# Where the moving tiles start and in which order the products of a k tile are issued; a loop written out

## The reference

```python
# first block
proj = rms_norm(x, g_mix) @ w_in                   # 2048 x 9216
...
x = x + merged @ w_out
h2 = rms_norm(x, g_ff)
x = x + square(relu(h2 @ w_ff1)) @ w_ff2           # 2048 x 8192, 8192 x 2048
# second block
h = modulate(rmsnorm(x, norm1_g), sh1, sc1)
q, k, v, f, hy = split_projection(h @ w_in_2)      # 2048 x 5120
kc, vc = split(hc @ w_in_2[:, 1024:3072], 2)       # the context, 256 rows too
...
x = x + g1 * (y @ w_out_2)
gate, up = split(modulate(rmsnorm(x, norm2_g), sh2, sc2) @ w_up, 2)   # 2048 x 11264
x = x + g2 * ((gelu(dwconv(gate)) * up) @ w_down)                     # 5632 x 2048
```

## Time and profile before

| | us |
|---|---|
| three runs, median | 2763.87 |
| three runs, lowest and highest | 2761.56, 2767.94 |
| the profiled execution, its own time | 2765.6 |
| its span, from the first to the last instruction | 2763.8 |
| TensorE busy | 2683.0 |
| VectorE busy | 1899.2 |
| ScalarE busy | 1178.4 |
| mean granted clock of TensorE | 0.983 |
| read from HBM | 553.57 MB |

### The profile page before, as it was taken

How to read it: one execution, slowest core, us unless ns; L and a number is a source line. 1 busy time by engine, 2 the same in 40 slices (tenths; PEclk the granted TensorE clock), 3 DMA queues, 4 the chain that set the end, 5 groups by cost and what they waited for, 6 DMA issues and landing times. The chain is left out here.

```text
span 2763.8 us, 51119 instructions
## 1 busy us (share of the span) xinstructions
PE 2683.0 (97%) x21116; PEld 2587.0 (94%) x21116; DVE 1899.2 (69%) x2409; ACT 1178.4 (43%) x1228; POOL 0.2 (0%) x4
## 2 busy tenths in 40 slices
PE   7999999998999999999999999999899999999998
PEld 7989999998999999999999899859899999999998
DVE  7778877886888788888872236756666665656566
ACT  4666554434543444343432233333444443434343
POOL 0000000000000000000000000000000000000000
PEclk9999999999999999999999999999999999999999
DMA  7666666675888888878743253404455554545453
GB/s 281 223 226 220 212 232 237 237 244 191 268 269 278 274 280 273 279 274 275 272 171 100 99 166 126 154 20 145 146 192 189 184 192 160 186 166 185 167 184 106
DMA packets 282686, 558.37 MB, mean 202 GB/s; under 512 B 10408, under 2 KB 16841, under 8 KB 282057
## 3 DMA queue, kind: packets, MB, share of 16 engines
q1 hardware_dynamic: 282104, 553.60, 58.5%
q10 hardware_dynamic: 400, 2.11, 0.3%
HBM read 553.57 MB, written 2.10 MB: 201 GB/s over the span
## 5 line engine op out<-in xcount | busy, mean ns | idle before, releaser
L882 DVE TENSOR_TENSOR WL<-RAW,WH 128x1024 fp32r<-128x1024 f32 x840 | 1018.9, 1223 | 699.8 <-ACT WH L477 692.1
L477 ACT ACTIVATE WH<-RAW 128x1024 fp32r<-128x1024 f32 x840 | 890.9, 1063 | 1404.1 <-PE PS L1591 1280.2
L1589 PE MATMUL PS<-XH,WH 128*128 128x256 f32 x4288 | 1215.9, 284 | 41.1 <-issue 27.5
L1590 PE MATMUL PS<-XL,WH 128*128 128x256 f32 x4288 | 1205.6, 281 | 0.0
L1591 PE MATMUL PS<-XH,WL 128*128 128x256 f32 x4288 | 1204.9, 281 | 0.0
L1589 PEld LDWEIGHTS PS<-XH,WH 128*128 128x128 f32 x4288 | 815.2, 190 | 46.9 <-issue 33.3
L1590 PEld LDWEIGHTS PS<-XL,WH 128*128 128x128 f32 x4288 | 815.6, 190 | 1.2 <-issue 0.7
L1591 PEld LDWEIGHTS PS<-XH,WL 128*128 128x128 f32 x4288 | 815.0, 190 | 0.0
L1589 PE MATMUL PS<-HH,WH 128*128 128x256 f32 x1728 | 482.8, 279 | 0.4 <-DVE X L1192 0.4
L1590 PE MATMUL PS<-HL,WH 128*128 128x256 f32 x1728 | 482.3, 279 | 0.0
L1591 PE MATMUL PS<-HH,WL 128*128 128x256 f32 x1728 | 482.2, 279 | 0.0
(11 more groups left out here) (240 smaller groups left out, 1888.2 us busy)
## 6 DMA issues: line engine op xcount, KB each, us to landing
RAW<-in_w_ff SPq DMA_DIRECT2D x128, 1024.0 KB, 5.4
RAW<-in_w_in SPq DMA_DIRECT2D x112, 1024.0 KB, 5.1
RAW<-in_w_up SPq DMA_DIRECT2D x88, 1024.0 KB, 4.8
adab<-in_ada_w SPq DMA_DIRECT2D x128, 512.0 KB, 4.7
RAW<-in_w_down SPq DMA_DIRECT2D x44, 1024.0 KB, 5.0
ada1b<-in_ada_w SPq DMA_DIRECT2D x64, 512.0 KB, 5.9
RAW<-in_w_out SPq DMA_DIRECT2D x32, 1024.0 KB, 5.0
RAW<-in_w_oa SPq DMA_DIRECT2D x8, 1024.0 KB, 5.1
```

The source lines that it names most:

```text
L477: A(WH[:, c.base % 2, hs], RAW[:, c.base % SLOTS, hs], ACT.Copy).then_inc(hi_done, 1)
L882: tt(WL[:, b, hs], RAW[:, c.base % SLOTS, hs], WH[:, b, hs].bitcast(f32), ALU.subtract)\
L1589: MM(out[:, f, :], wh, xh, start=first and f % 2 == 0, stop=False, skip_group_check=True)
L1590: MM(out[:, f, :], wh, xl, start=False, stop=False, skip_group_check=True)
```

## The change

Three things. The tiles that move through TensorE (`XH`, `XL`, `HH`, `HL`) start 32 bytes later, on odd multiples of 32 bytes, and with them all that shares their place; `CON` moves by 64 bytes to make room. `ws` issues, for each of the three products of a k tile, the four column blocks in the order 0, 2, 1, 3 before it goes to the next product. The loop of the second feed-forward is written out on all four engines: eight more calls of `ff2_step` with fixed chunk numbers.

```diff
@@
-FF2_ITERS = (STEPS2 - 3) // 2
@@
-        XH = at("XH", [P, KC, T], 80 * K + 64, f32r)
-        XL = at("XL", [P, KC, T], 96 * K + 64, f32r)
-        HH = at("HH", [P, 2, FT, T], 112 * K + 64, f32r)
-        HL = at("HL", [P, 2, FT, T], 120 * K + 64, f32r)
-        NT = at("NT", [P, KC, T], 112 * K + 64)
-        CON = 128 * K + 64
+        XH = at("XH", [P, KC, T], 80 * K + 96, f32r)
+        XL = at("XL", [P, KC, T], 96 * K + 96, f32r)
+        HH = at("HH", [P, 2, FT, T], 112 * K + 96, f32r)
+        HL = at("HL", [P, 2, FT, T], 120 * K + 96, f32r)
+        NT = at("NT", [P, KC, T], 112 * K + 96)
+        CON = 128 * K + 128
@@
-        t1 = 112 * K + 64
+        t1 = 112 * K + 96
@@
-        fcl = at("fcl", [P, TT, 2 * T], 80 * K + 64)
+        fcl = at("fcl", [P, TT, 2 * T], 80 * K + 96)
...
@@ SP; ScalarE, VectorE and TensorE alike
-            with sp.Fori(0, FF2_ITERS) as i:
-                ff2_step(Place(2, i, 2))
-                ff2_step(Place(3, i, 2))
+            for j in range(2, STEPS2 - 1):
+                ff2_step(Place(j))
@@ ws
-                for f in range(FT):
-                    cs = slice(f * P, (f + 1) * P)
-                    wh, wl = WH[:, b, kk, cs], WL[:, b, kk, cs]
-                    MM(out[:, f, :], wh, xh, start=first and f % 2 == 0, stop=False, skip_group_check=True)
-                    MM(out[:, f, :], wh, xl, start=False, stop=False, skip_group_check=True)
-                    ins = MM(out[:, f, :], wl, xh, start=False, stop=last, skip_group_check=True)
+                for n, (w, x) in enumerate(((WH, xh), (WH, xl), (WL, xh))):
+                    for f in (0, 2, 1, 3):
+                        ins = MM(out[:, f, :], w[:, b, kk, f * P:(f + 1) * P], x, start=first and n == 0 and f % 2 == 0,
+                                 stop=last and n == 2, skip_group_check=True)
```

More of the change, by code:

```diff
@@ L246, in build_program @@
         SM = at("SM", [P, KC, T], AR + 8 * K)
-        fcl = at("fcl", [P, TT, 2 * T], 80 * K + 64)
-        fcd = at("fcd", [P, 2, P], 84 * K + 64)
-        fU = at("fU", [P, FNG, 2 * T], 88 * K + 64)
+        fcl = at("fcl", [P, TT, 2 * T], 80 * K + 96)
+        fcd = at("fcd", [P, 2, P], 84 * K + 96)
+        fU = at("fU", [P, FNG, 2 * T], 88 * K + 96)
         KS = at("KS", [P, 2, 5, HW], AR + 24 * K)
@@ L252, in build_program @@
         YS = at("YS", [P, 4, HW], AR + 48 * K)
[L253 to L258, removed]
+        hSD = at("hSD", [P, 2, 2, TT, HW], 80 * K + 96)
+        dec = at("dec", [P, 2, TT, HW], 96 * K + 96)
+        Ef = at("Ef", [P, TT, 6 * P], 104 * K + 96)
+        pz = at("pz", [33, T], 110 * K + 96)
+        w1h = at("w1h", [33, 64], 111 * K + 96)
+        w2h = at("w2h", [64, 64], 111 * K + 96 + 512)
         w3h = at("w3h", [64, 2048], t1)
@@ L861, in _ @@
             ff2_step(Place(1))
-            with act.Fori(0, FF2_ITERS) as i:
-                ff2_step(Place(2, i, 2))
-                ff2_step(Place(3, i, 2))
+            for j in range(2, STEPS2 - 1):
+                ff2_step(Place(j))
             for s in range(4):
@@ L1550, in _ @@
             ff2_step(Place(1))
-            with dve.Fori(0, FF2_ITERS) as i:
-                ff2_step(Place(2, i, 2))
-                ff2_step(Place(3, i, 2))
+            for j in range(2, STEPS2 - 1):
+                ff2_step(Place(j))
             c, q = Place(C_END - 4), Place(Q_END - 4)
@@ L1999, in _ @@
             ff2_step(Place(1))
-            with pe.Fori(0, FF2_ITERS) as i:
-                ff2_step(Place(2, i, 2))
-                ff2_step(Place(3, i, 2))
+            for j in range(2, STEPS2 - 1):
+                ff2_step(Place(j))
             for s in range(SLOTS):
```

## The result

| | before, us | after, us |
|---|---|---|
| median of the timed runs | 2767.82 | 2751.60 |
| lowest, highest of 12 runs each | 2759.04, 2772.18 | 2730.04, 2757.25 |
| the profiled execution, its own time | 2765.6 | 2750.69 |
| its span | 2763.8 | 2748.9 |

The ratio after to before is 0.9943 [0.9925, 0.9962]: faster by 0.57%, some 16 us, where 92 us had been forecast and the range ended at 2737. Here is the page of the kernel after: busy time by engine, the clock in 40 slices, and two of the costliest groups.

A forecast was written before the change was run, and what follows sets the result against it. TensorE's own matmul pace was taken as the bound. From the profiled 2765.6 us, -59.5 (parity), -2.7 (`tok`), 0 (order) and -29.7 (loop) sum to -91.9, giving 2673.7; the median, 1.7 lower, 2672 us; range 2640 to 2737.

The forecast's parts named there:

- (1) Parity: `ws` matmuls with XH, XL, HH, HL: odd multiples of 32 bytes give 113.3 ns instead of 116.7, -59.5 us.
- three paces: `ws` matmuls in the earlier trace: XH at 116.7 ns apart, MH at 117.7, CH at 113.3.
- rival C: `ws` matmuls: odd tiles share two paces, half at 113.3 and half at 117.7 ns; 2713 us, chance 0.14.
- (2) `tok`: 672 `tok` matmuls with XH: odd place gains 4.0 ns each, -2.7 us.
- (3) The order: Product order in `ws`, bank changing after each matmul: 0 us, bounds -24 and -4 us against +48 us.
- D: `ws`: the order helps too, down to the weight loads' pace, 112 ns; 2644 to 2648 us, chance 0.14.
- E: `ws`: 16,000 added bank changes cost time; at 3 ns each without parity gain 2782 us, chance 0.07.
- (4) The loop: Second feed-forward's loop written out: stalls and half clock at three boundaries go, -29.7 us.
- The cover: VectorE, ScalarE and DMA work behind the matmuls: still hidden at the faster pace, priced 0.
- The rule against it: Skill's statement on TensorE: separate read ports, loads steal no bandwidth; tile places would change nothing, leaving the loop's gain alone.
- rival B: Whole kernel: neither parity nor order does anything, only the loop gains; 2734 us, chance 0.16.

## Why the prediction was right or wrong

**(1) Parity, -59.5 us forecast, +16 us measured: wrong, and this is the step that failed.** The price per matmul was real, 113.3 for 116.7, and so were the three paces. The variable was read wrongly. `CH` and `XH` in the earlier trace rows differ in parity, but also in their distance from the weights, 192 and 32 modulo 256. I took the one property that the change alters, and put the new `XH` with `CH`. It came to lie at 64, whose usual pace is 117.8. `MH`, as odd as `CH` and at 117.7 in the earlier trace rows, stood against it from the start. The prediction priced it for all matmuls only as the lower bound of this term, "it would cost 18,048 x 1.0 = +18 us" (rival C took it for half of them), and gave that outcome neither a rival nor a chance. With the loop it makes 2764 - 30 + 18 = 2752, and 2751.6 was measured. So close a match is luck, since that sum starts 4 us below the median of before in the same comparison and leaves out what `MH` and `CH` lost. A bound that has a row of its own in the same trace is a rival.
By the paces, the moved tiles cost 18,048 x 1.1 = 20 us, `MH` and `CH` at 120.0 instead of 113.3 or 117.8 another 4 to 8, and that is more than the 16 measured. TensorE also ran at half clock for less time in the profile with the tiles alone (68 us in all) than in that of before (98 us), but this differs from execution to execution, also 91 us with the order alone. Over all their timed runs the mean granted clock is 0.986 with the tiles alone and 0.984 before, some 11 us less at half clock; at 116.7 and 213 ns a matmul that is worth about 5 us, an estimate, which brings the 24 to 28 down to 19 to 23. The measured interval ends at 22.

**(2) `tok`, -2.7 us forecast, nothing gained.** In the profile after, the starts with `XH` still lie 233.3 ns apart; spans of nine with `CH` mostly give 226.7 (228.9 in the earlier trace rows). Here as there parity was not the variable, and the distance was: with `XH` the starts of `tok` lie 233.3 ns apart at 32, 64 and 112, 228.9 at 192 and 226.7 at 0. So the best of these distances for `tok` is the one at which `ws` takes 120.0.

**(3) The order, 0 forecast: right.** 1.0002 [0.9991, 1.0012] puts it between -2.5 and +3.3 us for 16,000 more changes of bank, at most 0.2 ns each. The upper bound of 3 ns (+48 us) and the lower one, the pace of the loads (-24 us), are both gone, and rivals D and E with them.

**(4) The loop, -29.7 us forecast, -31.8 measured: right.** The windows of the kernel after show straight code at clock 1.00 where the earlier trace rows had 0.96, and the stalls by "issue" fell by 17.7 us in six pieces. The half clock that followed them is gone too: 39 matmuls at each of three places, at 213 ns instead of 116.7, are another 11 us, and the two make 29 of the 31.8, within the interval.

**The cover: right.** VectorE at 1899.7 us and ScalarE at 1178.3 did not change, and even at 113.3 nothing waited anew.

**The rule against it.** The prediction set the trace against the Trainium skill (TensorE: Matmul & The Clock Gate, step 1 of "Step-by-step: what each phase is for"), by which the streaming operand and the loads have ports of their own. By that rule place would change nothing, and the time would have been rival B's 2734. The runs bear out neither B nor my reading: with every other engine still, place alone moved the pace from 113.3 to 123.3 ns. Whatever the ports are, the two operands don't go independently of their distance.

**Of the rivals,** none gave the result. C had the two paces right, but between 113.3 and 117.8 at equal shares; the kernel after has 19 of some 907 groups at the better one. Had it been priced with `MH`'s pace alone, its 2752 would have been in the range.

**What stays open:** what picks the pace where a distance has two; what sets the pace where the two moving tiles lie at different distances; why two of the 12 timed executions of the kernel after took 2730 us, which a better share of 113.3 would explain but which no profile caught; and what in the chip has a period of 256 bytes.

## What to carry to other kernels

Where TensorE's pace is the time, measure the pace of a matmul stream as the distance between starts, and compare it across tiles that differ only in place: here the distance between the moving tile and the weights, modulo 256 bytes, is worth up to 4% of a whole kernel, for no instruction at all. Sweep the distance in a small kernel of TensorE alone before moving anything, with repeats, since a distance may have two paces, and for each form of matmul, since `ws` and `tok` have different best distances; and list what else tells two rows apart before taking one property for the cause. A loop on TensorE whose branch back takes 6 us, as the one with 1152 matmuls and as many loads did here, costs some 10 us a turn and is worth writing out.

## What the runs showed of the hardware that was not expected

- The pace of float32r matmuls of 256 columns with a load of weights each depends on the distance between the operands in SBUF modulo 256 bytes, from 113.3 ns (112 bytes) to 123.3 ns (4 bytes), with all other engines idle. Which paces a distance has does not depend on the absolute place, tried at five places of the weights and with the moving tiles 40 K further. This holds where all moving tiles keep the same distance.
- With 512 moving columns and the activations stationary, the same distances give 226.7 ns (0), 228.9 (192) and 233.3 (32, 64 and 112).
- Distances of 32, 64 and 192 bytes have two paces each, chosen at a break and kept until the next one, in one case for some 6,200 matmuls; 112 had only one in 24 of 24 segments. In the whole kernel at 112 it was the pace of 877 of 971 groups of `XH`.
- Taking the PSUM banks in turn costs and gives nothing: 1.0002 [0.9991, 1.0012].
- TensorE's branch back took 6.0 us with a body of 1152 matmuls and as many loads, and 0.2 us with 768 of each. Writing the long one out gave 31.8 us for three boundaries. The Trainium skill (Runtime: NRT & Kernel Launch, "Instruction fetch mechanics") gives TensorE room for 2048 instructions, and 1536 and 2304 fall on the two sides of it, so the trace agrees with that figure. The section also says that a taken branch stalls when its target isn't in the current window of two pages; were these the blocks of 256 instructions that it names, both bodies would be too long, and the 0.2 us does not bear that out. No other length was tried here, so that the length makes the 6 us is likely and not shown.
